# A decoder layer on one core: head logits before values, four sample products in one run, a split later in the tail

## The reference

```python
x = x + 0.5 * swiglu_ffn(x, ffn1_norm, ffn1_w_in, ffn1_w_out)      # hidden 2816
h = rmsnorm(x, mix_norm)
proj = h @ w_in                                                    # 2048 columns: u, q, k, v, qm
y_pool = pool_mixer(u, ...)                                        # 4 windows, cumsum form
y_moba = moba_attention(rotary(rmsnorm(q)), k_all, v_all, pos)     # 8 heads x 64; samples: 1024 cached tokens
y_mem  = mem_attention(rmsnorm(qm), mk, mv)                        # 4 heads x 64, 256 memory tokens
x = x + concatenate([y_pool, y_moba, y_mem]) @ w_out
x = x + 0.5 * swiglu_ffn(x, ffn2_norm, ffn2_w_in, ffn2_w_out)
```

## Time and profile before

| | us |
|---|---|
| median of 3 runs | 560.4 (559.86 to 560.5) |
| the profiled execution, its own time | 560.33 |
| its span, first to last instruction | 558.5 |
| TensorE busy in the span | 551.9 (99%) |
| VectorE, ScalarE busy | 398.8, 269.4 |

### The profile page before, as it was taken

How to read it: one execution, slowest core, us unless ns; L and a number is a source line. 1 busy time by engine, 2 the same in 40 slices (tenths; PEclk the granted TensorE clock), 3 DMA queues, 4 the chain that set the end, 5 groups by cost and what they waited for, 6 DMA issues and landing times.

```text
span 558.5 us, 13391 instructions
## 1 busy us (share of the span) xinstructions
PE 551.9 (99%) x5075; PEld 514.3 (92%) x5075; DVE 398.8 (71%) x715; ACT 269.4 (48%) x425; POOL 17.7 (3%) x24
## 2 busy tenths in 40 slices
PE   9999999999999999999999999999999999999997
PEld 9999999999899998566777779999999999999997
DVE  4686878885688877899936685689777777664444
ACT  6843465444543337344535885475444344433330
POOL 1000000000000003000000000140000000000000
PEclk9999999999999999999999999999999999999999
DMA  8799999784567664899999984567756666465523
GB/s 242 220 262 303 268 316 282 239 248 152 191 217 273 209 205 154 283 344 383 361 315 377 374 301 137 164 179 196 211 171 188 186 171 191 133 226 181 188 75 79
DMA packets 137480, 128.40 MB, mean 230 GB/s; under 512 B 10936, under 2 KB 108879, under 8 KB 137431
## 3 DMA queue, kind: packets, MB, share of 16 engines
q1 hardware_dynamic: 134703, 127.24, 72.6%
q10 hardware_dynamic: 2736, 0.61, 0.5%
HBM read 125.12 MB, written 2.83 MB: 229 GB/s over the span
## 4 chain that ended last, share of the span: by engine, by line
PE 83%; DVE 7%; DMA 5%; ACT 2%; issue 1%; SPq 1%; DVEq 0%; ACTq 0%
PE banks L1506 24%; PE banks L1507 24%; PE banks L1508 24%; DMA raw<-in_ffn_w_in 4%; PE banks L1666 3%; PE banks L1514 2%; PE banks L1940 2%; DVE w_lo L1022 2%; PE banks L1638 1%; PE banks L1867 1%; PE banks L1891 1%; DMA page_ids<-in_page_table 1%; DVE banks L1436 0%; DVE kp L1138 0%; ACT w_hi L702 0%
## 5 line engine op out<-in xcount | busy, mean ns | idle before, releaser
L702 ACT ACTIVATE w_hi<-raw 128x1024 fp32r<-128x1024 f32 x158 | 166.4, 1058 | 195.7 <-PE banks L1508 157.6
L1022 DVE TENSOR_TENSOR w_lo<-raw,w_hi 128x1024 fp32r<-128x1024 f32 x158 | 193.8, 1232 | 74.2 <-ACT w_hi L702 73.2
L1506 PE MATMUL banks<-x_hi,w_hi 128*128 128x264 f32 x752 | 214.1, 285 | 0.2 <-DVE h_tmp L1066 0.2
L1507 PE MATMUL banks<-x_lo,w_hi 128*128 128x264 f32 x752 | 213.0, 283 | 0.0
L1508 PE MATMUL banks<-x_hi,w_lo 128*128 128x264 f32 x752 | 213.0, 283 | 0.0
L1506 PEld LDWEIGHTS banks<-x_hi,w_hi 128*128 128x128 f32 x752 | 141.6, 188 | 0.8 <-issue 0.7
L1507 PEld LDWEIGHTS banks<-x_lo,w_hi 128*128 128x128 f32 x752 | 141.7, 188 | 0.0
L1508 PEld LDWEIGHTS banks<-x_hi,w_lo 128*128 128x128 f32 x752 | 141.0, 188 | 0.0
L1506 PE MATMUL banks<-h_hi,w_hi 128*128 (+1 forms) x352 | 100.2, 285 | 0.1
L1508 PE MATMUL banks<-h_hi,w_lo 128*128 (+1 forms) x352 | 100.1, 284 | 0.0
L1507 PE MATMUL banks<-h_lo,w_hi 128*128 (+1 forms) x352 | 100.0, 284 | 0.0
(11 more groups left out here) (287 smaller groups left out, 503.9 us busy)
## 6 DMA issues: line engine op xcount, KB each, us to landing
raw<-in_ffn_w_in SPq DMA_DIRECT2D x86, 512.0 KB, 4.8
raw<-in_ffn_w_out SPq DMA_DIRECT2D x44, 512.0 KB, 3.8
kv<-in_cache_k SPq DMA_DIRECT2D x56, 256.0 KB, 4.9
kv<-in_cache_v SPq DMA_DIRECT2D x48, 256.0 KB, 6.3
raw<-in_w_in SPq DMA_DIRECT2D x12, 512.0 KB, 5.7
late_slot<-in_cache_v SPq DMA_DIRECT2D x16, 256.0 KB, 5.3
raw<-in_w_out SPq DMA_DIRECT2D x8, 512.0 KB, 7.2
raw<-in_mem_w_kv SPq DMA_DIRECT2D x4, 512.0 KB, 3.5
```

What stands on the lines that cost most here:

```text
L702: act.activation(w_hi[:, n % RING, :], raw[:, n % RING, :], ACT.Copy).then_inc(hi_ready, 1)
L1022: vec.tensor_tensor(w_lo[:, n % RING, :], raw[:, n % RING, :], w_hi[:, n % RING, :].bitcast(F32), ALU.subtract).then_inc(lo_ready, 1)
L1506: pe.matmul(out, lhs[0], rhs[0], start=start, stop=False)
L1507: pe.matmul(out, lhs[0], rhs[1], start=False, stop=False)
```

## The change

Only the order of tokens behind unit 10 is changed: `S` 12 to 15 leave their places behind units 11, 12, 13 and 14 and stand in one run behind `V` 3, behind unit 14; `HA` k now stands ahead of `V` and `PV`; `V` 0 and `V` 1 stand together behind unit 12, `V` 4 moves behind unit 15; `MG` 0 to 2 move one place back; `NQ` 5 and `NV` 5 move behind `HE` 7 and `V` 5; `WL` 16 moves from the end of unit 15 behind `HV` 7 in the tail; in the tail `HB` 10 and 11 stand ahead of `M` 1.

```diff
-            11: {2: [("A", 4)], 3: [("ET", 4)], 4: [("ET", 5), ("S", 12), ("WL", 13), ("W", 14)]},
+            11: {2: [("A", 4)], 3: [("ET", 4)], 4: [("ET", 5), ("WL", 13), ("W", 14)]},
...
+                 4: [("HA", 2), ("PV", 1), ("HY", 0), ("V", 3), ("S", 12), ("S", 13), ("S", 14), ("S", 15), ("ES", 3), ("YR", 0),
+                     ("HM", 4), ("HM", 5), ("HE", 4), ("HE", 5)]},
```

More of the change, by code:

```diff
@@ L412, in layer @@
             10: {0: [("A", 3)], 1: [("NS", 4), ("NG", 4)], 4: [("W", 13)]},
[9 rows of a table removed]
[11 rows of a table added]
         }
-        TAIL = ([("T", 4), ("NQ", 6), ("HV", 6), ("HV", 7), ("POOL", 0), ("MG", 4), ("HB", 6), ("HT", 6), ("HB", 7), ("HT", 7), ("MG", 5), ("NV", 6), ("ND", 5),
+        TAIL = ([("T", 4), ("NQ", 6), ("HV", 6), ("HV", 7), ("WL", 16), ("POOL", 0), ("MG", 4), ("HB", 6), ("HT", 6), ("HB", 7), ("HT", 7), ("MG", 5), ("NV", 6), ("ND", 5),
                  ("ND", 6), ("NS", 5), ("NS", 6), ("PV", 3), ("MG", 6), ("HA", 4), ("HM", 8), ("HM", 9), ("EXP", 0), ("POOL", 1), ("HE", 8), ("HE", 9), ("MG", 7),
                  ("QT", 1), ("V", 6), ("HV", 8), ("HV", 9), ("HA", 5), ("HM", 10), ("HM", 11), ("HY", 1), ("HB", 8), ("HT", 8),
[2 rows of a table removed]
[2 rows of a table added]
                  ("WL", 18), ("YR", 2), ("MIX", 0), ("W", 19), ("Y", 2), ("MIX", 1), ("WL", 19), ("CAT", 1), ("MX", 0), ("MX", 1), ("MIX", 2), ("MIX", 3)])
```

## The result

The changed kernel took 567.15 us (median of five runs, 563.92 to 568.18) against 560.4: 1.0108 of the time before, 95% interval 1.0091 to 1.0125. Run again later beside others it took 565.8 against 560.58, 1.0084 (1.0063 to 1.0105). The forecast was 561.6 with a range up to 563.2. So the sign was right, and four fifths of the loss were not in the sum. Of the eleven runs of the change in the two sittings, the three with a mean clock of 1.0 or 0.999 took 563.13 to 564.25, the eight at 0.997 or less 565.4 to 568.18.

The account below looks back on a forecast made before the run. TensorE, busy in 99% of the span, was taken as the bound. Packing at -1.3 us and waits at +2.6 us gave +1.3 on 560.33, so 561.6 us, range 560.4 to 563.2.

Parts of the forecast that it names:

- (2): `HA` 0, with only one part of unit 12 now ahead, waits for ScalarE's copy to `kT`: +0.41 us.
- (6): Tail: `V` "mem" waits for ScalarE's copy of what `M` 1 turned, no longer hidden by eight transposes: +0.55 us.
- Term (4): Behind unit 14: new waits at `Y` 0, heads 4 and 5 and `MG` 2, less the wait of `MG` 1: +1.23 us.
- Term (1): Turns of `A` 5 wait for VectorE's `p_own`, returning the time freed by moving `S` 12: +0.72 us.
- term (3): Row maxima of heads 0 to 3 start earlier, so six transposes take 0.94 instead of 1.15: -0.2 us.
- term (5): `WL` 16 leaves the place ahead of `HV` 6; waits at the transposes and `MG` 5 and 6 shrink: -0.1 us.
- changes of form: Fewer switches on TensorE between full-width work and strips or halves, with shared runs, claimed to save 1.3 us.
- The shared runs: Equal tokens in one run save 0.38 us for four sample products and 0.13 for `V` 0 with `V` 1.
- The four excursions: Trips from full-width work into strips or halves fall from eight to four, 0.19 us each: 0.76 us saved.
- The DMA queue, costed at nothing, and its cover: SyncE issues w_out unit 0 10.8 us later, yet sample 6's pages land 1.1 us ahead of `V` 6: no cost.
- The gate: Rival: `V` 6 or `V` 5 waits for pages behind SyncE's stop, 0.5 to 2 us on top, about 562.6; chance 0.22.
- Wrong: `V` 6 starting on a DMA's landing: Sign at `V` 6 in the profile that the forecast fails and the w_out gate decides.

Follow-up runs that it names:

- e14: The change with SyncE issuing w_out unit 0 behind the values of sample 5, and unit 2 behind those of sample 6: 561.62 us, ratio 1.0017.
- e11: Kernel before with `S` 12 to 15 in one run behind `V` 3, values of sample 5 and `mv` issued ahead of w_out unit 0: 561.77 us.
- e2: Kernel before with only sample products 12, 13 and 14 moved to the place of 15, behind `V` 3: 564.08 us, ratio 1.0056.
- e4: Kernel before with one SyncE wait added: w_out unit 0 not issued before `V` 3 ends; TensorE's list untouched: 561.87 us, ratio 1.0022.
- e6: Kernel before with one SyncE wait added: w_out unit 0 not issued before the last sample product ends: 564.38 us, ratio 1.0055.
- e15: The change itself, unaltered, timed once more beside the others: 565.8 us.
- e12: Kernel before with SyncE stopped until the last sample product ends, values of sample 5 and `mv` issued ahead of the stop: 561.41 us, ratio 1.0011.
- e7: Kernel before with about thirty tokens reordered to leave no open TensorE waits, `S` 12 to 15 staying about in place: 559.32 us, ratio 0.9973.
- e8: e7 with w_out unit 2 issued behind the values of sample 6 instead of ahead of them: 559.82 us, ratio 0.9986.
- e9: Kernel before with only `WL` 16 moved, from the end of unit 15 to behind `HV` 7 in the tail: 559.78 us, ratio 0.9975.
- e10: The change with values of sample 5 and `mv` issued ahead of w_out unit 0, and `M` 1 back ahead of heads 10 and 11: 562.33 us.
- e16: Kernel before with a second reordering, fewer tokens than e7, including `V` 0 with `V` 1 and `WL` 16 behind `HV` 7: 560.0 us, ratio 0.9985.
- e3: The change with only SyncE's order altered: values of sample 5 and memory values issued ahead of w_out unit 0: 562.59 us, ratio 1.0045.
- e1: The change with sample products 12 to 15 back at their old places behind units 11 to 14: 560.89 us, ratio 1.0005.
- e5: Kernel before with only the tail's part: `M` 1 and unit 17's split behind the transposes of heads 10 and 11: 561.25 us, ratio 1.0012.
- e13: The change with `M` 1 back in place, w_out unit 0 behind sample 5's values and unit 2 behind sample 6's: 561.02 us, ratio 1.0012.

## Why the prediction was wrong

**The sum on TensorE came out near, in part by luck.** In e14, which has the change's list without the stop, it is 287.58 from `A` 4 to the end, +1.10 over before; the sum said +1.3. By parts: up to `V` 6 +0.20, `V` 6 to `V` 7 +0.28, `V` 7 to `V` "mem" +0.54, the rest of the way 0.08. Terms (2) and (6) are right to 0.02. Up to `V` 6 the sum had +0.8, and both of its sides were too large. The waits, counted from start to start, grow there by about 1.05 where 2.06 was written. Term (4) was 0.6 too large: `Y` 0 waits 0.33 for 0.47, heads 4 and 5 0.7 for 0.94, `MG` 2 0.33 for 0.56. Term (1) is 0.57 for 0.72, term (3) -0.32 for -0.2, and term (5), with the pooling products behind it, -0.24 for -0.1.

So the changes of form save only about 0.85 where 1.27 was written. The shared runs are right: the pair of value batches saves 0.11 for 0.13, and the four sample products with `V` 3 ahead of them 0.35 for 0.38 (1.75 + 1.86 now; 1.86, 0.56, 0.44, 0.55 and 0.55 before). The four excursions save about 0.4, not 0.76. The one at `S` 12 can be seen: its place gives back 0.57, not 0.75, since around the first pass of unit 12 the starts still stand 0.19 wider than elsewhere (277.42, 277.77, 278.08 in the trace of the change). Why is open. The two errors of waits and form cancel but for 0.6. That `V` 6 to `V` 7 grows by 0.28 was not in the sum: `HA` 5 waits 0.93 there, 0.65 before.

The prediction weighed a rule of the Trainium skill, "TensorEngine Tiling (Array Packing)", section Tiling Modes: changing the mode drains the array. The order with fewer modes does save in these traces, but it isn't the faster one: e11, which packs the samples, is slower than before.

**"The DMA queue, costed at nothing, and its cover" failed.** This step put the queue at nothing, with the pages of sample 6 landing 1.1 us ahead of `V` 6. They land 3.3 us behind TensorE's arrival there. The step had the place and the mechanism, and named the point from which it decides; it was wrong in three ways.

The first is the landing. The text took 7.86 MB at 377 GB/s and 1.6 us until the first bytes, 22.4 us from the issue of unit 0 to the landing at `V` 6. It takes 26.4 (302.71 to 329.06) in the change, and 26.5, 26.9, 27.4 and 27.2 in e2, e4, e6 and e15. The windows of the change divide the 4.0 us. From the issue to 314.0 the engines move 265 GB/s instead of 377: 1.26 MB less, 3.4 us, where 1.6 stood in the sum, 1.8 too little. The first bytes do move about 1.1 us behind the issue (no row of before shows the 1.6); what is slow is what follows. That SyncE hands over one page after another, eight pages or 2.1 MB in 6.17 us, at most 340 GB/s, fits that; it isn't tested by itself. The other half is the bytes. From the issue to the landing the engines move 329 GB/s, 8.67 MB, 0.8 more than was counted, which is 2.1 us at 377; in e4, where no hole stands, it is 9.60 MB. So other transfers share the engines with those that were counted. By the times of issue they are the pages of sample 7, issued from 322.44 on, before those of sample 6 have landed, and in e4 also the memory keys, still on their way; which transfer had the extra bytes the windows don't show. The pages came 3.9 us behind the forecast; the cover was 1.1, and TensorE was there 0.6 earlier than counted: 3.9 - 1.1 + 0.6 = 3.4 from start to start, of which the row shows 3.30 as idle.

The second is the clock. Nothing in the text says that a stand of TensorE costs more than its length. It does here: `V` 6 to `V` 7 is 5.70 when `V` 6 is late at full clock (e2), 7.33 in e4 and e6, 8.33 and 8.43 in the two profiles of the change. So 1.6 to 2.7 go on top. Against that, 0.93 of `V` 6 to `V` 7 (6.63 in e14) is waiting that a late `V` 6 absorbs. Sum for the profiled execution: 3.38 more up to `V` 6, 1.70 more to `V` 7, 5.1 of the 6.16, and 1.1 for the list.

The third is the chance. The gate had 0.22 and a price of 0.5 to 2. With a cover of 1.1 us behind a queue that was computed at its best rate from a standing start, it should have been the likeliest case. "A restart 1.5 us slower than I think would show one for one": the landing was 4 later.

**What would show it.** "Wrong: `V` 6 starting on a DMA's landing" is what the profile has. The issue at 301 (302.71 less 1.69), the hole, and all the waits named as "right" are there too, so those signs could not tell the forecast from the gate; a value run of 128 matmuls takes 3.61, under the bound of 3.7.

**What stays open:** why e12 has two runs of twelve with a fallen clock (its ScalarE waits 0.24 for unit 0 in the profiled execution; those two runs have no profile), what makes unit 14 stand in e7 and e8, and which share of the slow landing is SyncE's pace of issue.

## What to carry to other kernels

When a compute step moves, look for the queue that waits on it, and cost what is queued behind that wait at the rate of a queue that starts empty (265 GB/s over the first 11.3 us here, against 377), with the bytes that are queued behind it as well. A moved step that frees a buffer should be followed by a look at the issue order: here, putting the values of sample 5 ahead of the blocked fetch and those of sample 6 ahead of w_out unit 2 (e14) gave back 4 of 5 us for no instruction. And a new wait of TensorE of the size seen here, 1.8 us and more, is to be priced with the chance of a fallen clock, 1.6 to 2.7 us here.

The version that came out best is e7 (0.9973, with all of its moves) or e9 (0.9975, with one token moved); both beat the kernel before and the change.

## What the runs showed of the hardware

A stand of TensorE can pull its clock to the lower level, and does so in some runs and not in others of the same kernel. In the profiles the clock fell at stands of 1.83 (e10), 1.99 (e4), 3.30 and 3.77 us (the change) and 4.44 (e6), and didn't at 2.45 (e2), 2.25 (e8), 1.12 (e16) and 0.84 (e3), so the length of the stand alone doesn't say. In the change it fell while TensorE stood; in e4 and e6 it fell 0.6 and 0.9 us after `V` 6 had started. In e4, e6 and e10 the low stretch is about 3.4 us long, in both profiles of the change twice that. In e4:

```profile
326.00:328.00 2.00, 0.84 (x28) 0.85 (x32) 1.90 (x8) 2.00 (x7) 0.00 (x0) 0.93 1.06 388
328.00:330.00 2.00, 2.00 (x44) 1.59 (x36) 0.67 (x3) 0.11 (x1) 0.00 (x0) 0.50 1.06 397
330.00:332.00 2.00, 2.00 (x19) 1.33 (x12) 0.19 (x1) 0.00 (x0) 0.00 (x0) 0.72 1.02 404
332.00:334.00 2.00, 2.00 (x32) 1.37 (x34) 1.93 (x5) 1.60 (x5) 0.00 (x0) 1.00 1.05 397
```

Counted over the runs, the mean clock was 0.997 or less in 4 of 5 and 4 of 6 of the change, 6 of 9 of e6, 2 of 6 of e2, 3 of 12 of e4, 5 of 12 of e10, 3 of 11 of e3, 3 of 12 of e8, 2 of 12 of e12 and 1 of 8 of e7, and in none of e1, e5, e9, e11, e13, e14 and e16. The Trainium skill, "TensorE: Matmul & The Clock Gate", Part 1, says that the window in which TensorE's activity is watched runs free and isn't reset by the start of a kernel, so that the same kernel differs from run to run. That the same kernel differs agrees: e4 has 9 runs of one kind and 3 of the other. The reason is not shown by these runs.
